# A hybrid mixer and mixture-of-experts kernel: routers fed from the raw residual, expert counts computed earlier, and two weight buffers moved in SBUF

## The reference

```python
x = x + mix @ w_out                                   # block 1: RWKV-7 and gated linear attention mixers
x = x + hier_moe(rmsnorm(x, ln2_w), ...)              # 32 experts of width 512, each token takes 2
x = rmsnorm(x, ln_f_w)
# block 2: attention, dense SwiGLU (width 3584), then
x = x + z[..., :1024] * sigmoid(z[..., 1024:])        # S5 state-space layer, z = y @ w_glu
x = moe_swiglu(x)                                     # 8 experts of width 3584, each token takes 2

hf = rmsnorm(x, ln2_w)
coarse, fine = hf @ w_coarse + b_coarse, hf @ w_fine + b_fine
gsel = argmax(coarse); pf = softmax(fine[gsel]); top_p, top_e = top_k(pf, 2)
# every expert: (silu(xb @ w_gate[e]) * (xb @ w_up[e])) @ w_down[e], weighted and summed by token
rmsnorm(x, w) = x * rsqrt(mean(x * x) + 1e-6) * w
```

## Time and profile before

| | us |
|---|---|
| median of 3 runs | 2148.38 |
| lowest, highest | 2144.46, 2149.61 |
| profiled execution, its own time | 2143.83 |
| span of its trace | 2142.1 |
| busy: PE, DVE, ACT | 1912.3, 705.8, 274.4 |
| granted TensorE clock, mean | 0.951 |

### The profile page before, as it was taken

One profiled execution on the slowest core, in us unless ns is written; L12 is line 12 of the kernel. 1 busy time (PEld: TensorE's weight loads), 2 busy tenths in 40 slices (PEclk: granted clock), 3 DMA queues, 4 the chain that ended last, 5 costly groups with the idle time before them and its releaser, 6 DMA issues.

```text
span 2142.1 us, 29684 instructions
## 1 busy us (share of the span) xinstructions
PE 1912.3 (89%) x12966; PEld 998.4 (47%) x12966; DVE 705.8 (33%) x1426; ACT 274.4 (13%) x480; POOL 54.7 (3%) x36
## 2 busy tenths in 40 slices
PE   7999987666767679899999998999999999999998
PEld 5789952222222246477776665333343433333332
DVE  3585554233333346511536352001011112121112
ACT  2241101111111123401010020000000000000000
POOL 0034100000000000000000000000000000000000
PEclk9999988888787989999999998999999999999999
DMA  6301179999999962053342107999999999999997
GB/s 232 123 7 43 50 311 415 430 430 431 430 430 431 430 277 118 1 240 143 132 169 106 79 2 296 430 431 431 430 431 430 430 424 425 430 430 427 429 430 306
DMA packets 51573, 646.44 MB, mean 302 GB/s; under 512 B 8272, under 2 KB 10576, under 8 KB 12656
## 3 DMA queue, kind: packets, MB, share of 16 engines
q1 hardware_dynamic: 51440, 644.48, 71.5%
HBM read 643.41 MB, written 1.05 MB: 301 GB/s over the span
## 4 chain that ended last, share of the span: by engine, by line
PE 79%; DMA 11%; DVE 5%; issue 3%; ACT 1%; SPq 0%; DVEq 0%; ACTq 0%
PE low L875 40%; PE high L875 35%; DMA slot<-in_moe_w_up 11%; PE low L1507 1%; PE low L884 1%; DVE hact L2376 1%; DVE xn L2376 0%; DVE hT L2376 0%; DVE Rf L2636 0%; DVE xn L2380 0%; DVE sg L2376 0%; DMA x_sb<-in_x 0%; ACT hT L1955 0%; DVE xn L2417 0%; PE low L1624 0%
## 5 line engine op out<-in xcount | busy, mean ns | idle before, releaser
L875 PE MATMUL low<-slot,xgh 128*64 128x512 f32 x1120 | 256.8, 600 | 8.3 <-DMA slot<-in_moe_w_up 7.2
L875 PE MATMUL high<-slot,hTs 128*64 128x512 f32 (+2 forms) x1232 | 253.5, 596 | 0.6 <-DVE hTs L2966 0.6
L875 PE MATMUL high<-slot,xgT 128*32 128x512 f32 (+1 forms) x1520 | 222.0, 637 | 34.7 <-issue 22.8
L875 PE MATMUL low<-hT,slot 128*128 128x256 f32 x960 | 210.9, 381 | 2.0 <-DVE hT L2376 2.0
L875 PE MATMUL low<-slot,xgT 128*32 128x512 f32 (+2 forms) x848 | 173.7, 670 | 31.6 <-issue 19.1
L875 PEld LDWEIGHTS low<-hT,slot 128*128 128x128 f32 x960 | 183.0, 191 | 30.2 <-issue 2.9
L875 PEld LDWEIGHTS high<-slot,hTs 128*64 128x64 f32 (+2 forms) x1232 | 80.4, 132 | 166.4 <-issue 166.4
L875 PEld LDWEIGHTS high<-slot,xgT 128*32 128x32 f32 (+1 forms) x1520 | 68.9, 122 | 185.3 <-issue 185.2
L875 PEld LDWEIGHTS low<-slot,xgh 128*64 128x64 f32 x1120 | 77.2, 137 | 151.6 <-issue 144.1
L875 PEld LDWEIGHTS low<-slot,xgT 128*32 128x32 f32 (+2 forms) x848 | 56.0, 139 | 138.6 <-issue 129.9
L875 PE MATMUL high<-hT,slot 128*128 128x256 f32 (+1 forms) x448 | 100.1, 385 | 0.8 <-DVE hT L2376 0.8
(11 more groups left out here) (441 smaller groups left out, 1849.9 us busy)
## 6 DMA issues: line engine op xcount, KB each, us to landing
slot<-in_moe_w_down SPq DMA_DIRECT2D x88, 2048.0 KB, 18.9
slot<-in_moe_w_up SPq DMA_DIRECT2D x88, 2048.0 KB, 18.3
slot<-in_moe_w_gate SPq DMA_DIRECT2D x88, 2048.0 KB, 15.5
slot<-in_dffn_w_gate SPq DMA_DIRECT2D x7, 2048.0 KB, 8.3
slot<-in_dffn_w_up SPq DMA_DIRECT2D x7, 2048.0 KB, 13.0
slot<-in_dffn_w_down SPq DMA_DIRECT2D x7, 2048.0 KB, 8.4
slot<-in_w_in_tiles SPq DMA_DIRECT2D x6, 2048.0 KB, 8.3
slot<-in_att_w_in SPq DMA_DIRECT2D x3, 2048.0 KB, 14.3
```

The source lines that it names most:

```text
L875: return nc.tensor.matmul(o, l, r, start=start, stop=stop)
```

## The change

1. **Routers.** PE transposes the raw `x_sb` in four pieces of 512 columns (`turn_piece`), interleaved with the last w_out (or S5 output) piece; DVE applies the gain into `xgT` (`piece_turned`); the router product runs on that, tile 0's before the last w_out piece is finished, and `logits1` or `logits2` multiply it by `1 / rms`. ACT takes over the squares (`square_piece`) and the writing of `xn` (`scale_tile`).
2. **Counts and ranks.** PE starts tile 0's products before tile 1's mask is there (`chosen_two` instead of `ranked`). Counts go to a PSUM bank of their own; in moe2 they come first and `in_order` follows at once. The routing weights (`two_weights`) are computed after ranks, choice and flag.
3. **Branch.** In moe1 `places(0)` stands ahead of `either` on DVE, and PE waits for it ahead of its own `either`. The dense path, not taken here, makes its `hT` again.
4. **Buffers.** Slots 6 and 7 lie at the start of the expert layers' SBUF region, over other tiles of the mixer, and SP issues their loads after the mixer's `rw1_y` products and the bonus fold, ahead of the wait for w_out. Some other tiles are moved to make room.

```diff
+            sp.wait_ge(v_filled, V.at["rw1_y"] + 2)
+            weight(N_E1 - 1, 0, g1)
+            sp.wait_ge(rw_folded, 2)
+            weight(N_E1 - 1, 1, u1)
             sp.wait_ge(mixed, 2)
             sp.wait_ge(wout_filled, 4)
             weight(0, 0, g1)
             weight(0, 2, d1)
-            weight(N_E1 - 1, 0, g1)
-            weight(N_E1 - 1, 1, u1)
...
-            turn("ln2", 0)
-            mixed_half(1, 1, range(4)).then_inc(wout.filled, 1)
+            for j in range(2):
+                wout.landed(pe, j)
+                turn_piece("ln2", 0, j)
+            mixed_half(1, 1, range(2))
+            wout.landed(pe, 2)
+            turn_piece("ln2", 1, 0)
+            pe.wait_ge(router_in, 32)
+            route("route1", "ln2", 0, 0, 36)
+            mixed_half(1, 1, range(2, 4)).then_inc(wout.filled, 1)
...
-                pe.wait_ge(ranked, 1 if x is moe1 else 2)
...
+                pe.wait_ge(chosen_two, seen + 1)
                 mm(b[:, 0:n], cst("before"), msk[:, 0, 0:n])
+                mm(b[:, n:2 * n], cst("ones"), msk[:, 0, 0:n], True, False)
+                mm(ahead[:, 0:n], cst("ones"), msk[:, 0, 0:n], True, False)
+                pe.wait_ge(chosen_two, seen + 2)
...
+                V.landed(pe, max(rank_item, count_item))
+                pe.wait_ge(normed, TT * NORMS.index("ln2" if x is moe1 else "moe") + TT)
                 S_.landed(pe, x.last_s)
                 if x is moe1:
                     gather_quad(0)
+                    quads1.ring.landed(pe, quads1.ring.at["x", 0] + 1)
...
+            route("route1", "ln2", 1, 0, 36, (0,))
+            wout.landed(pe, 3)
+            turn_piece("ln2", 1, 1)
+            route("route1", "ln2", 1, 0, 36, (1,))
...
+            def square_piece(t, c):
+                cols = slice(c * 512, c * 512 + 512)
+                f(xn[:, t, cols], x_sb[:, t, cols], ACT.Square, accum_out=st[:, 2 * t + c:2 * t + c + 1]
+                  ).then_inc(piece_squared, 1)
+            def scale_tile(name, t):
+                act.wait_ge(scaled_by, (0 if name == "ln2" else 2) + t + 1)
+                f(xn[:, t, :], x_sb[:, t, :], ACT.Copy, scale=st[:, 84 + t:85 + t]).then_inc(normed, 1)
...
+            for n in range(3):
+                add_mixed(n)
+            piece_turned("ln2", 0, 0)
+            piece_turned("ln2", 0, 1)
+            piece_mean("ln2", 0)
+            piece_turned("ln2", 1, 0)
+            piece_scale("ln2", 0)
             logits1(0)
             two_of_group(0)
+            add_mixed(3)
+            piece_turned("ln2", 1, 1)
+            piece_mean("ln2", 1)
+            piece_scale("ln2", 1)
             logits1(1)
             two_of_group(1)
...
+            ranks(moe1, V.at["rank1"])
+            choose_quad(0)
+            b = V.take(dve, V.at["count1"])
+            vec.tensor_reduce(cnt[:, 0:1], b[:, 0:N_E1], AXX, ALU.max).then_inc(V.emptied, 1)
...
+            two_weights(1, N_E1)
+            places(0)
             either(dve, moe1, False, half_scales(dense), quads, half_scales(gathered))
...
+            in_order(V.take(dve, V.at["count2"]))
+            ranks(moe2, V.at["rank2"])
+            by_order(rank, rank_o)
+            for k in mix2.gathers(-1):
+                choose_mixed(k)
+            enough_room()
+            two_weights(2, N_E2)
+            by_order(wexp, wexp_o)
             either(dve, moe2, True, dense, packed)
```

More of the change, by code:

```diff
@@ L1310, in dense @@
             def dense(x):
+                for t in range(TT):
+                    for j in range(2):
+                        b = psum[2 * t + j]
+                        for q in range(4):
+                            c = (4 * j + q) * P
+                            last = nc.tensor.transpose(b[:, q * P:q * P + P], xn[:, t, c:c + P], ident)
+                        last.then_inc(x.again_filled, 1)
+                pe.wait_ge(x.again_emptied, 4)
                 hid, out_ = (x.hid_filled, x.hid_emptied, 0), (x.out_filled, x.out_emptied, 0)
@@ L2848, in dense @@
             def dense(x):
+                for t in range(TT):
+                    for j in range(2):
+                        dve.wait_ge(x.again_filled, 2 * t + j + 1)
+                        tt(hT[:, 4 * j:4 * j + 4, t * P:t * P + P], psum[2 * t + j].rearrange("p (k c) -> p k c", k=4),
+                           spread(pcol("ln2" if x is moe1 else "moe", 4 * j, 4), P), ALU.mult).then_inc(x.again_emptied, 1)
                 dve.sem_inc(x.hid_emptied, 4)
@@ L3041, in packed, with places @@
                     add(k)
+            def places(g):
+                ring = quads1.ring
+                for j in range(2):
+                    b = ring.take(dve, ring.at["x", g] + j)
+                    tt(xgT[:, g % 2, 4 * j:4 * j + 4, :], b[:, :].rearrange("p (q c) -> p q c", q=4),
+                       spread(pcol("ln2", 4 * j, 4), P), ALU.mult).then_inc(ring.emptied, 1)
             def quads(x):
@@ L3051, in weigh @@
                     ins.then_inc(m.sel_weighted, 1)
-                def places(g):
-                    for j in range(2):
-                        b = ring.take(dve, ring.at["x", g] + j)
-                        tt(xgT[:, g % 2, 4 * j:4 * j + 4, :], b[:, :].rearrange("p (q c) -> p q c", q=4),
-                           spread(pcol("ln2", 4 * j, 4), P), ALU.mult).then_inc(ring.emptied, 1)
                 def halves(o, b, i, j):
@@ L3185, in choose_mixed, with ranks @@
                 ins.then_inc(m.sel_ready, 1)
[L3187 removed]
+            def ranks(x, item):
                 n = x.count
                 b = V.take(dve, item)
[L3191 to L3193 removed]
                 stt_(rank[:, :, 0:n], b[:, 0:2 * n].rearrange("p (t e) -> p t e", t=TT), 1.0, msk[:, :, 0:n],
@@ L3642, in _ @@
             logits2(1)
             two_of(2, 8, 1)
-            own.settle()
-            dve.sem_inc(ranked, 1)
-            dve.wait_ge(logit_exp, 4)
-            do(ts(st[:, 18:20], st[:, 18:20], 1.0, ALU.add))
-            do(vec.reciprocal(st[:, 20:22], st[:, 18:20]))
-            for t in range(TT):
-                top_two(0, 8, t, True)
-            ranks(2, moe2, V.at["rank2"])
+            in_order(V.take(dve, V.at["count2"]))
+            ranks(moe2, V.at["rank2"])
+            by_order(rank, rank_o)
```

246 lines of the change are left out of this document (140 added, 106 removed).

## The result

| us | before | changed |
|---|---|---|
| median of the timed runs | 2147.28 (4 runs, 2144.46 to 2149.61) | 2134.53 (4 runs, 2130.62 to 2136.17) |
| profiled execution, its span | 2143.83, 2142.1 | 2136.17, 2134.4 |
| granted TensorE clock, mean | 0.951 | 0.951 |

The ratio is 0.9935, 95% interval 0.9923 to 0.9948: 14.0 us of 2147 faster, beyond the 0.3% that can be told from no change; the two medians differ by 12.75. The forecast was 2135.7 with 12.7 gained. The two profiled executions differ by only 7.7: the one of before (2143.83) was faster than all four of its timed runs, and the changed one was the slowest of its four. So the profiles alone would mislead here, and further profiles of the unedited changed kernel, taken with the experiments, are needed.

The account below looks back on a forecast made before the run. The prediction took moe1's and moe2's weight streams (DMA), in moe2 PE too, as the bound, so only earlier starts help: moe1 -5.5 and moe2 -7.2 give -12.7, 2148.38 to 2135.7 us; 8-in-10 range 2129.5 to 2144.

Parts of the forecast that it names:

- Router of moe1: moe1, to tile 1's logits: new order brings them at 300.1 (full clock) or 301.0 (half) instead of 303.66; -3.1 us.
- Branch of moe1: moe1, gather's end to hidden(0): places ahead of DVE's branch, PE's branch exposed at 0.9; -1.1 us (-1.9 to +5.1).
- DVE's late branch: moe1 after expert 2's gate: DVE back late from its branch delays expert 0 against the stream; cost 0 to 2, taken 0.4.
- Rival (a): moe1 gives nothing: PE's branch costs DVE's 7.07 or DVE's late branch starves the stream; 2141.5 us, chance 0.16.
- Slots 6 and 7: moe1: 9.8 us of transfers move into the hole at 290 us; price if undone about 1.5 us.
- Head in all: Sum of moe1's terms, up to the issue of expert 2's gate: -5.5 us.
- Rival (d): Slower: PE enters moe2's first units at half clock, 26 us more less 7 of slack; 2155 us, chance 0.05.
- Router of moe2: moe2, value piece's end to tile 1's logits, 10.47 before: logits at 1288.4 or 1289.3; -4.9 us.
- Counts of moe2: moe2, logits to lineup: counts first, 5.46 becomes 3.0; -2.4 us.
- Middle: moe2's stream start: router -4.9, table loads +0.1, counts -2.4; -7.2 us (from -5 to -8.7).
- (b): moe2's gain halved by half clock and a stream not quite full; 2139.4 us, chance 0.10.
- (c): More than forecast: full clock holds through ranks and gathers of both stages, 4 us in all; 2131.5 us, chance 0.09.

Follow-up runs that it names:

- e7: Changed kernel with moe2's choice matrices, and so PE's gathers, put behind flag and routing weights; median 2130.62 us, ratio 0.9924.
- e12: The changed kernel unedited, run and profiled a third time; median 2132.00 us, ratio 0.9929 to the kernel before.
- e8: Changed kernel with filler products on PE in both routers' waits and 12 more ahead of the dense layer's second transposes; 2128.78 us, ratio 0.9914.
- e10: e8 with expert 31's two loads (slots 6 and 7) back behind the wait for w_out; median 2131.87 us, ratio 0.9926.
- e9: Changed kernel with places(0) behind DVE's branch again and PE's wait for it ahead of its own branch removed; 2132.46 us, ratio 0.9931.
- e3: Changed kernel with expert 31's two loads (slots 6 and 7) back behind the wait for w_out; median 2134.24 us, ratio 0.9951.
- e5_changed_again: The changed kernel unedited, run and profiled a second time; median 2131.29 us, ratio 0.9926 to the kernel before.
- e11: The same kernel as e8, run again beside the unedited changed kernel; median 2128.32 us, ratio 0.9911.

## Why the prediction was right, and where it was not

**What bounds the kernel.** Right that each stream can only end earlier by starting earlier: moe1 keeps its 428 and the tail its 842. Wrong that in moe2 "the end moves only if both start earlier". PE's 7.2 us of waits in 840 looked like a second bound; e7 shows that they aren't one. A small sum of waits says that PE is nearly busy, not that its start binds: the waits come where PE has caught up with the stream, so it had room before each.

**Router of moe1, -3.1.** Measured -3.2 in two profiles and -2.8 in the third, whose second half product took 1.43 (half clock): the two cases of the forecast, 300.1 or 301.0.

**Ranks of moe1, -1.7.** Measured 3.65 from logits to gather in two profiles, -1.9, and 3.43 in e12.

**Branch of moe1, -1.1.** Measured -0.8: 1.97 from the gather's end to the hidden product. PE's branch was put at 0.9 and the issue time there is 1.2 to 1.3, so it is cheap and visible. But the term's reason failed. DVE's 7.07 was taken as its branch's price, and the same branch stood for 3.08 to 3.37 us in the changed kernel; it depends on what DMA does meanwhile. e8 and e10 have the same PE timing, and the stall is 3.08 with the share at 0.02 and 5.56 with it at 0.98. The two transfers moved early took the traffic away from the branch, and e9 shows that then no move of `places` was needed. The Trainium skill, "Runtime: NRT & Kernel Launch", section on instruction fetch mechanics, has a taken branch outside the prefetched pages stall until a DMA has fetched its target. The trace agrees in that a stall stands there and that a weight stream lengthens it, which I had left out; that it is the fetch, no run shows.

**DVE's late branch, +0.4.** Measured 0: expert 2's down was issued 8.27 after its gate, expert 3's gate 12.06 after, as before, with a branch of 3.37 and not 7.07. Rival (a) is out.

**Slots 6 and 7.** "About 1.5 if undone": 1.7 to 1.9 in e3, 2.2 to 3.4 in e10. That they would be worth nothing in the kernel before was not run.

**Head in all, -5.5.** Measured -6.2 in e5_changed_again, and -3.1 and -3.5 in the other two. The sum of the terms holds where the clock does: -3.2 - 1.9 - 0.3 (gather) - 0.8. What failed is a size that stood nowhere in the sum: the half clock reaches further into the stage. It is worth 0.7 to 0.9 in the gather (6.47 to 6.66 against 5.74) and 1.7 in the hidden product (5.34 against 3.64). Rival (d) named this mechanism, but at moe2's first units and with 26 us; it is small and sits at moe1's first product. The first two products of moe2's units took 7.09 and 7.03, before 7.08 and 7.03.

**Router of moe2, -4.9.** -5.4 in the changed kernel's first profile, -5.8 in the two others (tile 1's logits 4.66 behind the router product). The loads feared for the squares did not come: cost 0 where I put 0.1.

**Counts of moe2, -2.4.** -2.1 and -2.6 (3.19 and 2.73 for 5.29).

**Middle, -7.2.** -7.8 and -7.9 in e5_changed_again and e12, -5.4 in the changed kernel's first. Of the 2.4 between it and e12, 1.6 arise at the start of the dense layer, between its loads at 915 and 950 us, where the first profile's clock was 0.51 from 920 to 925 us, and 0.9 in moe2's router and counts. A half clock stands there in e5_changed_again too (0.53 from 915 to 920 us), one stretch earlier, so that it is the clock's place that costs the 1.6 is argued and not shown. "The stretch from 765 to 1280 us shifted whole" holds to 0.1 us in two profiles and fails by 1.6 in the third.

**Sum.** -12.7 forecast, and the two medians of the result differ by 12.75. That closeness is luck: between the profiles of before and of e12, which start alike (259.31 and 259.29), it is -11.3, and by the ratios of the three groups with the unedited kernel -14.0, -15.9 and -15.2. The difference lies in before too, whose profiled run was faster than all its timed ones. Two small slips of the forecast change nothing: by its own terms the branch's upper bound is +5.0 and not +5.1, and rival (c) gives 2131.7 and not 2131.5. `lineup` was forecast near 1286.5 and stood at 1290.94, 1286.41 and 1287.75; expert 2's gate near 315.6 and stood at 318.78, 316.39 and 317.95. Of the rivals, (b) has no ground, as moe2 gave more than forecast; (c) is what e8 and e11 build by hand, with the dense layer's fillers added: 2.5 and 3.7 below the changed kernel, where it gave 4.

## What to carry to other kernels

When two chains feed two full streams, measure each chain from its own first instruction to the stream's first transfer and each stream from there to its end: the parts that stay the same tell you at once what not to look at, and one profile's scatter doesn't hide the gain. Work that doesn't wait for anything late (here expert 31's loads) is worth moving early even if its old place looked like a hole, because the queue in front of the critical transfer is what counts, and by e3 and e10 it counts for no less when the chain gets shorter. Before a move is made to hide a branch, see whether its price is its own or that of the transfers beside it.

## What the runs showed of the hardware

- The stall of DVE's branch to a far path was 3.08 to 3.37 us with DMA idle (ten profiles), 5.56 and 5.74 with a weight stream at full share (e10, e3), and 7.07 in the kernel before. The issue time before PE's hidden product, where its inline branch lies, was 1.23 in the changed kernel's chain.
- An unedited kernel's hidden product of 32 instructions took 3.64 in one profile and 5.34 in two, by which part of it fell at the 1.2 GHz level (granted clock 0.5) before the clock came back to 2.4 GHz. Forty filler products of 128 columns, in waits in which PE had nothing to do, kept it at 1.00 from 290 to 315 and from 905 to 935 us and were worth 2.5 and 3.7 us of 2131.
- From moe2's first transfer to the end it took 841.6 to 842.6 us in all 14 profiles, while the head of 56 to 59 us scattered by 3 with one and the same kernel.
